# Eight FFN layers: the second weight panel without its products of zeros, in the order of all other panels

## What is computed

```python
def rms_norm(x, g):
    y = xf * lax.rsqrt(jnp.mean(xf * xf, axis=-1, keepdims=True) + EPS)
    return (y * g.astype(jnp.float32)).astype(x.dtype)

def swiglu(h, w_gate_up, w_down):      # 1024 x 5632, 2816 x 1024, float32
    gate, up = jnp.split(h @ w_gate_up, 2, axis=-1)
    return (jax.nn.silu(gate) * up) @ w_down
...
x = x + swiglu(rms_norm(x, g), w_gate_up, w_down)
```

## Time and profile before

| | before |
|---|---|
| median of three runs | 2560.88 us (2559.19 to 2564.55) |
| the profiled execution | 2567.75 us, span 2565.9 us |
| TensorE busy | 2473.8 us, 96% of the span |
| VectorE busy | 1776.5 us, 69% |
| ScalarE busy | 1261.9 us, 49% |
| HBM traffic | 426.45 MB read, 167 GB/s over the span |
| mean granted TensorE clock | 0.984 of full |

### The profile page before, as it was taken

One profiled execution on the slowest core, in us unless ns is written; L12 is line 12 of the kernel. 1 busy time (PEld: TensorE's weight loads), 2 busy tenths in 40 slices (PEclk: granted clock), 3 DMA queues, 4 the chain that ended last, 5 costly groups with the idle time before them and its releaser, 6 DMA issues.

```text
span 2565.9 us, 54733 instructions
## 1 busy us (share of the span) xinstructions
PE 2473.8 (96%) x23246; PEld 2416.9 (94%) x23246; DVE 1776.5 (69%) x2304; ACT 1261.9 (49%) x1525; POOL 216.4 (8%) x246
## 2 busy tenths in 40 slices
PE   9999769999999899999999999999999999999998
PEld 8999659999999889999999999999999998999998
DVE  6988956666555666666666669976667667986665
ACT  6444535335666653354343346665334335575433
POOL 4000150003000100000000000600000000420000
PEclk9999979999999899999999999999999999999999
DMA  6553024555677735545545544434555554434553
GB/s 217 197 182 125 19 69 179 193 188 193 183 180 178 170 135 189 193 145 183 193 180 200 191 162 166 147 131 176 194 196 181 196 194 144 155 134 152 188 188 127
DMA packets 65855, 430.76 MB, mean 168 GB/s; under 512 B 8304, under 2 KB 11376, under 8 KB 15920
## 3 DMA queue, kind: packets, MB, share of 16 engines
q1 hardware_dynamic: 58592, 410.14, 44.6%
q0 software_dynamic: 6000, 17.46, 4.6%
q10 hardware_dynamic: 1120, 1.08, 0.2%
HBM read 426.45 MB, written 1.15 MB: 167 GB/s over the span
## 4 chain that ended last, share of the span: by engine, by line
PE 84%; DVE 9%; ACT 4%; issue 2%; DMA 0%; ACTq 0%; DVEq 0%
PE psum L2095 66%; PE psum L2087 3%; PE psum L2089 3%; PE psum L2088 3%; DVE w_lo L1363 2%; ACT w_hi L854 1%; PE psum L2341 1%; PE psum L2245 1%; PE psum L2490 1%; PE psum L2478 1%; DVE h L1412 1%; PE psum L2150 1%; DVE h_lo L1371 1%; PE psum L2468 1%; PE psum L2434 0%
## 5 line engine op out<-in xcount | busy, mean ns | idle before, releaser
L854 ACT ACTIVATE w_hi<-raw 128x2048 fp32r<-128x2048 f32 x387 | 741.5, 1916 | 843.0 <-PE psum L2095 809.4
L1363 DVE TENSOR_TENSOR w_lo<-raw,w_hi 128x2048 fp32r<-128x2048 f32 x387 | 888.0, 2295 | 374.8 <-ACT w_hi L854 374.6
L2095 PE MATMUL psum<-h_hi,w_hi 128*128 128x256 f32 x3952 | 784.8, 280 | 15.7 <-DVE h_lo L1437 9.6
L2095 PE MATMUL psum<-h_hi,w_lo 128*128 128x256 f32 x3952 | 777.9, 278 | 1.0 <-issue 1.0
L2095 PE MATMUL psum<-h_lo,w_hi 128*128 128x256 f32 x3952 | 777.4, 278 | 0.0
L2095 PEld LDWEIGHTS psum<-h_hi,w_hi 128*128 128x128 f32 x3952 | 599.7, 189 | 26.7 <-issue 19.3
L2095 PEld LDWEIGHTS psum<-h_hi,w_lo 128*128 128x128 f32 x3952 | 600.3, 188 | 0.0
L2095 PEld LDWEIGHTS psum<-h_lo,w_hi 128*128 128x128 f32 x3952 | 599.8, 188 | 0.0
L2095 PE MATMUL psum<-act_hi,w_lo 128*128 128x256 f32 x1408 | 275.2, 277 | 0.0
L2095 PE MATMUL psum<-act_hi,w_hi 128*128 128x256 f32 x1408 | 275.1, 277 | 0.0
L2095 PE MATMUL psum<-act_lo,w_hi 128*128 128x256 f32 x1408 | 275.1, 277 | 0.0
(11 more groups left out here) (360 smaller groups left out, 2936.0 us busy)
## 6 DMA issues: line engine op xcount, KB each, us to landing
raw<-in_panels SPq DMA_DIRECT2D x387, 1024.0 KB, 4.8
arena<-bias_by_distance POOLq DMA_DIRECT2D x32, 384.0 KB, 6.3
x<-in_x SPq DMA_DIRECT2D x2, 512.0 KB, 5.0
arena<-in_s_cbd POOLq DMA_DIRECT2D x4, 256.0 KB, 4.0
arena<-in_s_b SPq DMA_DIRECT2D x1, 1024.0 KB, 13.0
arena<-in_s_c SPq DMA_DIRECT2D x1, 1024.0 KB, 13.2
hidden<-in_s_cbd POOLq DMA_DIRECT2D x4, 256.0 KB, 2.9
arena<-arena POOLq DMA_DIRECT2D x32, 32.0 KB, 1.9
```

The costliest lines, as they stand in the source:

```text
L854: a.activation(w_hi[:, s, :], raw[:, s, :], ACT.Copy).then_inc(hi_ready, 1)
L1363: v.tensor_tensor(w_lo[:, s, :], raw[:, s, :], w_hi[:, s, :].bitcast(F32), ALU.subtract).then_inc(lo_ready, 1)
L2095: last = t.matmul(o[m], w[m][wi], xin[xi], start=start and xi + wi + m == 0, stop=stop and wi == 1, skip_group_check=True)
```

## The change

The FFN's second panel is called without `led`: its 48 matmuls are issued in the woven order, and the three products of zeros in each of the eight FFNs (four matmul instructions with their weight loads) are gone. All else is as before, the Fourier and GLU panels with their leads too.

```diff
@@ -2177,7 +2177,7 @@
                              zeros[:, :].unsqueeze(1).to_broadcast([P, 4, P]), start=True, stop=True)
                 t.wait_ge(sq_added, 3 * (st["hn"] - st["whole"]))
                 t.matmul(bank[SUMS_BANK[True]][:, 0:S], ones[:, :], h[:, 0], start=True, stop=True).then_inc(ss_ready, 1)
-                project(n0 + 1, 1, led=PACE)
+                project(n0 + 1, 1)
                 t.wait_ge(rms_ready, st["hn"] + 1)
                 with t.Fori(0, (FFC - 1) // 2) as i:
                     for c in (1, 2):
```

## The result

The changed kernel takes 2612.23 us (median of four runs, 2608.69 to 2615.38), the kernel before 2560.45 us beside it. The ratio is 1.0200, with a 95% interval of 1.0182 to 1.0218: 2.0% slower. The profiled execution took 2612.61 us (span 2610.8, mean granted clock 0.984 as before), 44.9 us over the profiled one of before.

The account below looks back on a forecast made before the run. TensorE, busy 96% of the span, was taken as the bound. Pace loss of 47.1 us less 3.7 us for dropped products of zeros gave net +43.4 us; counted from 2560.88 us, the forecast was 2604 us, range 2569 to 2613.

Parts of the forecast that it names:

- term 1: FFN second panels and loops: matmuls lose 4.44 ns each, 6.67 us per FFN, 47.1 us over seven FFNs.
- Mostly slow: Second panel's start behind L2179 without products of zeros: mostly at the slow pace, about one fast in six to eight.
- term 2: FFN second panels: dropping the three products of zeros gains 0.46 us per FFN, 3.7 us in all.
- no loop slow before: Starting case for the FFN loops: median run has all eight fast; with one still fast afterwards, seven turn slow, 2604 us.
- terms 3 and 4: FFN second panel: interleaving the halves costs nothing; ending 0.46 us sooner makes nothing late, slack 4.3 us or more.
- A: Rival: woven second panels fall into the fast pace by themselves in all or nearly all FFNs, 2549 to 2556 us; chance 0.16.
- B: Rival: mixed starts behind L2179, three to five FFNs land fast, 2570 to 2590 us; chance 0.12.
- C: Rival: pace comes from something in a whole run, not the products of zeros; only these go, 2557 us; chance 0.05.
- D: Rival: the FFN loop becomes bound by VectorE or a transfer; called excluded by the slack, no chance given.

Follow-up runs that it names:

- the first experiment: Against the changed kernel, the FFNs' second panels keep the order half by half but have no products of zeros: 2610.48 us, ratio 1.0195.
- the dose: Against the changed kernel: order half by half, no products of zeros in FFNs 1 to 4, second wide and narrow ones in FFNs 5 to 8: 2583.52 us.

## Why the prediction was right

**The time** was forecast as 2604 us, 1.7% slower, and came as 2612, 2.0% slower. That is inside the range of 2569 to 2613, but only just, and most of the miss lies in one choice, told below.

**The pace** (term 1 of the sum) was right in kind and size. Counted from matmul to matmul in the two traces, the distance from the third panel's first start to the loop's last one is 168.53 us before and 175.14 us after in each of FFNs 2 to 8, 6.61 us more, which is 1487 distances of 4.44 ns. In FFN 1 it is 175.14 us in both. "Mostly slow" was right too, but it came from counting other starts and not from a cause: eight of eight were slow behind L2179, where the rows had said about one fast in six to eight. In the ten traced kernels with no lead directly behind L2179 it is 76 of 80. The count itself had one class wrong. Of the 24 `mm3` runs that the prediction calls those with the weights stationary, 8 have the weights as moving operand, the one behind L2701 at 1684 among them. They run at the same two paces, so 120 ns is not the mark of moving weights; the 12 runs at 120 ns are all in the dilated mixer. The share of slow starts stays as it was.

**The leads** (term 2) were right. In FFN 8 the second real matmul behind L2179 starts 0.765 us after it with the first wide lead and 0.654 us without, so that lead costs 0.11 us, as assumed. The second wide one costs 0.11 to 0.12 and the narrow one 0.22, together 0.45 us for the 0.46 of the sum. Of this, 6.59 less 6.19, that is 0.40 us per FFN or 3.2 us in all, shows between L2179 and the third panel, because the last 11 distances of the second panel lost 4.44 ns each (0.05 us) in the same stretch.

**What the median had.** Here I chose wrongly. I saw that the profiled execution of before lay 6.9 us over the median and that this is one slow loop. But then I paired "no loop slow before" with "one fast after", so the two cancelled. All eight were slow after: eight loops at 6.61 us and 0.4 us more for FFN 2, less 3.2 us, is 50.1 us; the medians differ by 51.8 us. That the median execution of before had no slow loop was not traced. It fits that the two kernels whose profile has none took 2559.9 and 2560.9 us in it. The profiled executions differ by 44.9 us, where seven loops (46.3 us), the same 0.4 us, and the leads give 43.5 us. The other 1.4 us lies outside the loops and second panels: the stages in between differ by up to 3.3 us, one way and the other, from one trace to the other.

**Order and slack** (terms 3 and 4) held: the order costs nothing, as the kernel without leads in the old order shows, and no wait came up in a loop. The third panel's split ends 3.9 us or more before the panel starts, where it was 4.3.

**The rivals.** A (the start falls into the fast pace by itself) and B (mixed) didn't come about in the changed kernel; the woven kernel with a lone narrow lead, three loops of eight fast in its profile, looks like B. C (the pace has nothing to do with the leads) fell with the first experiment and the dose. D didn't occur.

**Where the reading was too simple.** "The narrow lead sets to fast nearly always" was true of the rows, 10 of 11, and wrong as a mechanism. I took the eleventh for chance. It was the only one that stood behind the other place in the cycle, and the kernel with the narrow lead alone failed in seven FFNs of its profile for the same reason. The forecast only had to say what happens without any lead, so it was luck that this error didn't touch it.

## What to carry to other kernels

In a TensorE-bound stretch compare the distance between starts across equal loops; two values for the same matmul at the same clock are a state, and the last interruption, with the place at which it falls, decides it for as long as nothing interrupts again. A few instructions that compute nothing can be worth many times their price there, so they have to be judged by the run behind them. And when a remedy works in 10 cases of 11, look at the eleventh before calling it luck: here it held the rule.

## What the runs showed of the hardware

- A dense run of fp32r matmuls of 128x128 by 128x256, each with its own weight load, has two lasting distances between starts at full granted clock, 113.33 and 117.78 ns. It kept the slow one for 1632 matmuls and the fast one for 1608 without a change.
- The slow one repeats after three matmuls (353.33 ns). A narrow lead ends it or not by its position in these three (76 of 76 at two of the places, 0 of 21 at the third): one matmul later cost 1.2% of the kernel, three later nothing.
- The Trainium skill, page "TensorE: Matmul & The Clock Gate", section on the gap of 56 ns, has one warm distance, an estimate of 109 ns here. The traces show it in no dense run of these matmuls.
- Behind the float32 matmul L2179 with nothing between, the run came out slow in all eight FFNs of the changed kernel and of the one without leads, and in 76 of 80 over ten traced kernels. What in the chip makes the three places, and what sets the place behind L2179, is not shown by any run here.
